# Attention with negated scores, the differential heads' norm moved among the units, and their rows combined before the division

## The reference, cut to what matters

```python
def diff_mixer(q, k, v, lam, lam_init, g_subln):
    ...
        logits = jnp.einsum('bqhcd,bshcd->bchqs', qb, k, preferred_element_type=jnp.float32) * scale
        logits = jnp.where(admissible[None, None, None], logits, -jnp.inf)
        p = jax.nn.softmax(logits, axis=-1)
        attn = p[:, 0] - lam * p[:, 1]
        return jnp.einsum('bhqs,bshe->bqhe', attn.astype(v.dtype), v)
    ...
    return rms_norm(out, g_subln) * (1.0 - lam_init)
...
mixed = jnp.concatenate([out_a, out_b], axis=-1)
x = x + jnp.einsum('bsc,cd->bsd', mixed, w_out[layer])
```

## Time and profile before

| | |
|---|---|
| median of 3 runs | 3076.5 us (3076.12 to 3080.77) |
| the profiled execution: its own time | 3079.2 us |
| its span | 3077.1 us |
| PE busy | 2821.8 us, 92% |
| DVE busy | 1800.8 us, 59% |
| ACT busy | 1132.6 us, 37% |
| granted PE clock, mean | 0.95 |

### The profile page before, as it was taken

How to read it: one execution, slowest core, us unless ns; L and a number is a source line. 1 busy time by engine, 2 the same in 40 slices (tenths; PEclk the granted TensorE clock), 3 DMA queues, 4 the chain that set the end, 5 groups by cost and what they waited for, 6 DMA issues and landing times.

```text
span 3077.1 us, 41761 instructions
## 1 busy us (share of the span) xinstructions
PE 2821.8 (92%) x16794; PEld 2132.6 (69%) x16794; DVE 1800.8 (59%) x3354; ACT 1132.6 (37%) x2024; POOL 151.4 (5%) x139
## 2 busy tenths in 40 slices
PE   7998977889999999999979976999999997899998
PEld 4887755775667667667637754788887764678887
DVE  4257866565677777777565787433334688443333
ACT  3323223222255556556513336322222325432222
POOL 0000000000012222212100000000000000000000
PEclk9998887889999999999999988999999997999999
DMA  6210002323368889899882200324222210222412
GB/s 222 83 57 19 1 1 72 115 58 142 120 262 337 345 349 357 344 359 347 311 328 99 83 7 1 117 69 130 70 86 105 83 62 1 83 69 76 137 52 72
DMA packets 180783, 433.08 MB, mean 141 GB/s; under 512 B 20131, under 2 KB 109542, under 8 KB 161254
## 3 DMA queue, kind: packets, MB, share of 16 engines
q1 hardware_dynamic: 161862, 396.72, 35.8%
q0 software_dynamic: 18720, 33.60, 2.9%
HBM read 426.56 MB, written 38.29 MB: 151 GB/s over the span
## 4 chain that ended last, share of the span: by engine, by line
PE 67%; DVE 10%; DMA 5%; ACT 3%; issue 2%; POOL 0%; SPq 0%; POOLq 0%; DVEq 0%; ACTq 0%
PE ps L298 15%; PE ps L299 15%; PE ps L300 15%; PE ps L2498 6%; DMA ring<-in_ew 2%; PE ps L2014 2%; PE ps L1506 2%; PE ps L2524 1%; DMA hg<-h_rows,idx 1%; DVE Pb L3405 1%; PE ps L2737 1%; PE ps L3137 1%; PE ps L2218 1%; DVE bi L3238 1%; DMA yr<-y_rows 1%
## 5 line engine op out<-in xcount | busy, mean ns | idle before, releaser
L2937 DVE TENSOR_TENSOR wf<-ring,wf 128x1024 fp32r<-128x1024 f32 (+1 forms) x152 | 181.6, 1197 | 336.8 <-ACT wf L2933 336.7
L2933 ACT ACTIVATE wf<-ring 128x1024 fp32r<-128x1024 f32 (+1 forms) x152 | 156.5, 1032 | 353.4 <-PE ps L300 353.4
L298 PE MATMUL ps<-hxh,wf 128*128 128x512 f32 x704 | 276.0, 392 | 2.8 <-DVE hxl L3082 2.8
L299 PE MATMUL ps<-hxl,wf 128*128 128x512 f32 x704 | 275.4, 391 | 0.0
L300 PE MATMUL ps<-hxh,wf 128*128 128x512 f32 x704 | 275.3, 391 | 0.0
L2436 DVE TENSOR_TENSOR spA<-ring,spA 128x1024 fp32r<-128x1024 f32 x156 | 184.5, 1222 | 102.7 <-ACT spA L2431 102.5
L2498 PE MATMUL ps<-ring,hdT 128*128 128x512 f32 x520 | 234.8, 594 | 0.8 <-issue 0.8
L2431 ACT ACTIVATE spA<-ring 128x1024 fp32r<-128x1024 f32 x156 | 157.7, 1053 | 50.1 <-DMA ring<-in_ew 42.9
L2436 DVE TENSOR_TENSOR spB<-ring,spB 128x1024 fp32r<-128x1024 f32 x104 | 124.3, 1222 | 68.4 <-ACT spB L2431 68.0
L2498 PEld LDWEIGHTS ps<-ring,hdT 128*128 128x128 f32 x520 | 93.8, 190 | 94.3 <-issue 91.4
L298 PEld LDWEIGHTS ps<-hxh,wf 128*128 128x128 f32 x704 | 133.2, 189 | 31.5 <-DVE hxl L3082 3.6
(11 more groups left out here) (615 smaller groups left out, 6222.5 us busy)
## 6 DMA issues: line engine op xcount, KB each, us to landing
ring<-in_ew SPq DMA_DIRECT2D x65, 2048.0 KB
ring<-in_ew SPq DMA_DIRECT2D x65, 1024.0 KB
ring<-in_w_in SPq DMA_DIRECT2D x17, 2048.0 KB, 7.8
ring<-in_w_gate SPq DMA_DIRECT2D x20, 1024.0 KB, 5.5
ring<-in_w_up SPq DMA_DIRECT2D x20, 1024.0 KB, 8.0
ring<-in_w_down SPq DMA_DIRECT2D x16, 1024.0 KB, 5.0
adaw<-in_ada_w SPq DMA_DIRECT2D x24, 512.0 KB, 6.2
ring<-in_w_out SPq DMA_DIRECT2D x6, 2048.0 KB, 7.8
```

The lines of the kernel that those rows point to most:

```text
L298: pe.matmul(o, lhs[0], rhs[0], start=start, stop=False)
L299: pe.matmul(o, lhs[0], rhs[1], start=False, stop=False)
L2933: act.activation(item_part(n)[0], item_raw(n), ACT.Copy).then_inc(*w_hi.inc(n))
L2937: v.tensor_tensor(item_part(n)[1], item_raw(n), f(item_part(n)[0]), ALU.subtract).then_inc(*w_lo.inc(n))
```

## The change

- `top` scales the scores by -0.125 and takes the minimum, so that no negation follows; the exponential gets scale -1.
- A differential unit is combined without division: `p0 + p1 * (sum0 * -lam / sum1)`; its row sum 0 stays in `esum`. The norm takes the factor: mean squares are multiplied twice by 1/`esum`, and the final scale once.
- Squares of the differential output stand in DVE's steps 21 to 24, the root in ACT's step 25, the scale in steps 27 to 31, the transposes in PE's steps 32 and 33, two of the four copies with gain in ACT's step 33.
- The first two weight splits of `W_out` stand in ACT's steps 17 and 18 and DVE's steps 25 and 26, in other buffers of `wf`.
- Behind the last unit ACT copies k = 0, 1, then the last two tiles with gain, then k = 2, 3, a split and k = 4 to 7. The output projection's first products wait for each tile alone.

```diff
+            nsq = sb("nsq", [128, 4, 128], c=s1)
+            esum = sb("esum", [128, 2, 16], c=s1)
...
-        s = wr[:, m % 2] if kind == "in" else wf[:, m % 4]
+        s = wr[:, m % 2] if kind == "in" else wf[:, (m + 2) % 4]
...
-        for i in range(4):
-            pe.wait_ge(*n_mul.val((l, i)))
-            for h in range(4):
-                m = pe.transpose(ps[i][:, h * 128:(h + 1) * 128], ob[:, i, h * 128:(h + 1) * 128], ident)
-            m.then_inc(*n_T.inc((l, i)))
+            for i in {32: (0, 1), 33: (2, 3)}.get(s, ()):
+                pe.wait_ge(*u_max.val((l, 31)))
+                pe.wait_ge(*n_mul.val((l, i)))
+                for h in range(4):
+                    m = pe.transpose(ps[i][:, h * 128:(h + 1) * 128], ob[:, i, h * 128:(h + 1) * 128], ident)
+                m.then_inc(*n_T.inc((l, i)))
 
     def attn_act(act, l):
+        n0 = first_of[l, "out"]
+
+        def rows_T(i0):
+            for i in (i0, i0 + 1):
+                act.wait_ge(*n_T.val((l, i)))
+                act.activation(ym_(l)[:, 4:8, i * 128:(i + 1) * 128], v4(ps[i][:, :]), ACT.Copy, scale=gsc[:, l:l + 1]).then_inc(*n_y.inc((l, i)))
...
-                    m = act.activation(p_, p_, ACT.Exp, bias=stt_[:, s % 4, 2 + c:3 + c], accum_out=stt_[:, s % 4, 4 + c:5 + c])
+                    m = act.activation(p_, p_, ACT.Exp, scale=-1.0, bias=stt_[:, s % 4, c:c + 1],
+                                       accum_out=esum[:, 0, s:s + 1] if UNITS[s][2] and c == 0 else stt_[:, s % 4, 4 + c:5 + c])
...
-        n0 = first_of[l, "out"]
-        for n in range(n0, n0 + 2):
-            split_hi(act, n)
+            if s in (17, 18):
+
+                act.wait_ge(*u_qk.val((l, 15)))
+                split_hi(act, n0 + s - 17)
+            if s == 25:
+                act.wait_ge(*n_sum.val(l))
+                act.activation(nrm[:, 1, :], nrm[:, 0, :], ACT.Sqrt, bias=EPS6, scale=1.0 / 128).then_inc(*n_sd.inc(l))
+            if s == 33:
+                rows_T(0)
         act.wait_ge(*u_out.val((l, 31)))
-        for k in range(4):
+        for k in range(8):
+            if k == 4:
+                act.wait_ge(*n_y.val((l, 3)))
+                split_hi(act, n0 + 2)
             act.activation(hx[0][:, k, :], ym_(l)[:, k, :], ACT.Copy).then_inc(*y_hi.inc((l, k)))
...
+            if k == 1:
+                rows_T(2)
...
             for c in range(2):
                 v.tensor_tensor_reduce(out=Pb[:, u % 4, c, 0:ns], in0=ps[2 * (u % 2) + c][:, 0:ns],
-                                       in1=zb[:, 512 - ns:512] if diff or i == 0 else bi[:, i - 1, 0:ns], scale=0.125, scalar=-3e38,
-                                       op0=ALU.add, op1=ALU.max, accum_out=s_[:, c:c + 1]).then_inc(*V.inc())
-            v.wait_ge(*V.val())
-            v.tensor_scalar(s_[:, 2:4], s_[:, 0:2], -1.0, None, ALU.mult).then_inc(*u_max.inc((l, u)))
+                                       in1=zb[:, 512 - ns:512] if diff or i == 0 else bi[:, i - 1, 0:ns], scale=-0.125, scalar=3e38,
+                                       op0=ALU.add, op1=ALU.min, accum_out=s_[:, c:c + 1]).then_inc(*(u_max.inc((l, u)) if c else V.inc()))
...
-            v.reciprocal(s_[:, 6:8], s_[:, 4:6]).then_inc(*V.inc())
-            v.wait_ge(*V.val())
             if diff:
-                v.tensor_tensor(s_[:, 7:8], s_[:, 7:8], lms[:, l, 7:8], ALU.mult).then_inc(*V.inc())
-                v.tensor_scalar(p0, p0, s_[:, 6:7], None, ALU.mult).then_inc(*V.inc())
+
+                v.reciprocal(s_[:, 7:8], s_[:, 5:6]).then_inc(*V.inc())
                 v.wait_ge(*V.val())
-                v.scalar_tensor_tensor(out=p0, in0=p1, scalar=s_[:, 7:8], in1=p0, op0=ALU.mult, op1=ALU.add).then_inc(*u_nrm.inc((l, u)))
+                v.scalar_tensor_tensor(out=s_[:, 6:7], in0=esum[:, 0, u:u + 1], scalar=s_[:, 7:8], in1=lms[:, l, 7:8], op0=ALU.mult,
+                                       op1=ALU.mult).then_inc(*V.inc())
+                v.wait_ge(*V.val())
+                v.scalar_tensor_tensor(out=p0, in0=p1, scalar=s_[:, 6:7], in1=p0, op0=ALU.mult, op1=ALU.add).then_inc(*u_nrm.inc((l, u)))
...
+        def squares(i):
+
+            v.wait_ge(*u_out.val((l, 4 * i + 3)))
+            v.wait_ge(*V.val())
+            for h in range(4):
+                o_, n = ob[:, i, 128 * h:128 * h + 128], 4 * i + h
+                m = v.tensor_tensor_reduce(out=nsq[:, h, :], in0=o_, in1=o_, scale=1.0, scalar=0.0, op0=ALU.mult, op1=ALU.add,
+                                           accum_out=nrm[:, 0, n:n + 1])
+            m.then_inc(*V.inc())
+            if i == 3:
+
+                v.reciprocal(esum[:, 1, :], esum[:, 0, :]).then_inc(*V.inc())
+                for k in range(2):
+                    v.wait_ge(*V.val())
+                    v.tensor_tensor(nrm[:, 0, :], nrm[:, 0, :], esum[:, 1, :], ALU.mult).then_inc(*(n_sum.inc(l) if k else V.inc()))
...
+            if 21 <= s < 25:
+                squares(s - 21)
+            if 25 <= s < 27:
+                split_lo(v, n0 + s - 25)
+            if s == 27:
+                v.wait_ge(*n_sd.val(l))
+                v.reciprocal(nrm[:, 0, :], nrm[:, 1, :]).then_inc(*V.inc())
+                v.wait_ge(*V.val())
+                v.tensor_tensor(nrm[:, 0, :], nrm[:, 0, :], esum[:, 1, :], ALU.mult).then_inc(*V.inc())
+            if 28 <= s < 32:
+                if s == 28:
+                    v.wait_ge(*V.val())
+                i = s - 28
+                v.tensor_tensor(v4(ob[:, i, :]), v4(ob[:, i, :]), bc(nrm[:, 0, 4 * i:4 * i + 4], 128), ALU.mult).then_inc(*n_mul.inc((l, i)))
+        for k in range(8):
             v.wait_ge(*y_hi.val((l, k)))
             v.tensor_tensor(hx[1][:, k, :], ym_(l)[:, k, :], f(hx[0][:, k, :]), ALU.subtract).then_inc(*y_lo.inc((l, k)))
...
+            if k == 3:
+                split_lo(v, n0 + 2)
...
-                if hf == 0 and kp == 0:
-                    pe.wait_ge(*n_y.val((l, 3)))
                 for i in range(4):
+                    if hf == 0 and kp == 0:
+                        pe.wait_ge(*n_y.val((l, i)))
                     m = part(hf, kp, i)
```

More of the change, by code:

```diff
@@ L3416, in normal @@
             v.wait_ge(*u_exp.val((l, u)))
-            v.reciprocal(s_[:, 6:8], s_[:, 4:6]).then_inc(*V.inc())
-            v.wait_ge(*V.val())
             if diff:
-                v.tensor_tensor(s_[:, 7:8], s_[:, 7:8], lms[:, l, 7:8], ALU.mult).then_inc(*V.inc())
-                v.tensor_scalar(p0, p0, s_[:, 6:7], None, ALU.mult).then_inc(*V.inc())
+                v.reciprocal(s_[:, 7:8], s_[:, 5:6]).then_inc(*V.inc())
                 v.wait_ge(*V.val())
-                v.scalar_tensor_tensor(out=p0, in0=p1, scalar=s_[:, 7:8], in1=p0, op0=ALU.mult, op1=ALU.add).then_inc(*u_nrm.inc((l, u)))
-            else:
+                v.scalar_tensor_tensor(out=s_[:, 6:7], in0=esum[:, 0, u:u + 1], scalar=s_[:, 7:8], in1=lms[:, l, 7:8], op0=ALU.mult,
+                                       op1=ALU.mult).then_inc(*V.inc())
+                v.wait_ge(*V.val())
+                v.scalar_tensor_tensor(out=p0, in0=p1, scalar=s_[:, 6:7], in1=p0, op0=ALU.mult, op1=ALU.add).then_inc(*u_nrm.inc((l, u)))
+            else:
+                v.reciprocal(s_[:, 6:8], s_[:, 4:6]).then_inc(*V.inc())
+                v.wait_ge(*V.val())
                 v.tensor_scalar(p0, p0, s_[:, 6:7], None, ALU.mult).then_inc(*V.inc())
                 v.tensor_scalar(p1, p1, s_[:, 7:8], None, ALU.mult).then_inc(*u_nrm.inc((l, u)))
+        n0 = first_of[l, "out"]
+        def squares(i):
[11 more added lines that the diff above has]
+                    v.tensor_tensor(nrm[:, 0, :], nrm[:, 0, :], esum[:, 1, :], ALU.mult).then_inc(*(n_sum.inc(l) if k else V.inc()))
         rest = IDX[sum(IDX_DVE):]
```

## The result

The changed kernel takes 3061.17 us (median of 4 runs, 3054.74 to 3066.3) beside 3078.64 us (4 runs, 3076.12 to 3083.41): a ratio of 0.9943, interval 0.993 to 0.9957, 17.5 us less. Forecast were 25.6 us less, 3051 with a range from 3044 to 3060. The direction was right and the median lies just outside the range. Of the 10.2 us between 3051 and 3061.17, 2.1 come from the base: the forecast started from 3076.5, and the kernel before has 3078.64 with its fourth run.

A forecast was written before the change was run, and what follows sets the result against it. DVE bounds the differential units, a ring of waits the selective ones, serial work the tail. Per layer -6.4 + 3.0 - 10.7 + 1.3 = -12.8, two layers -25.6: from 3076.5 to 3051 us, range 3044 to 3060.

The forecast's parts named there:

- rival of 0.03: Output projection begins and stays at low clock: all gain gone from 27% of it, 3144 us if all; chance 0.03.
- sign of failure: Forecast fails if the clock is low in wide differential units, or stretch two grows by more than 6 us per layer.
- The price list: Times of the old tail's work groups, used to price work moved among selective units, such as 0.9 us per squares group.
- Differential units: First attention stretch: negation and pass over p0 save 8.0 us of DVE, PE takes back 1.6; net -6.4 per layer.
- Selective units and drain: Second stretch: added work 4.8 less 1.6 for the negation, taken as +3.0 per layer; 16 transposes in the drain add 2.0.
- Tail: Behind the last unit: 14.6 us removed, 1.9 stays for copies and subtraction; with 2.0 for transposes, net -10.7 per layer.
- norm: Norm behind the output projection: a serial square-root table load between square and root, +1.3 us per layer.
- The rival with twice the time per load: Three table loads per layer on the path hold ACT 1.3 us more each: +7.8, 3059 us; chance 0.04.

The follow-up runs named there:

- table ahead: Changed kernel plus one square root of a constant behind the output projection's last weight split, loading the root's table early: 3055.98 us, ratio 0.9935.
- weight splits behind: Changed kernel with the first two splits of W_out moved back behind the last unit, on ACT and DVE: 3063.89 us, ratio 0.9946.

## Why the prediction was wrong

**The step that failed is the clock.** It said that the projection starts in a high clock because "only 2 us of idle time precede it", and held a low clock there for a rival of 0.03 that stays low throughout. It starts high, falls 1 us later and comes back 3 to 4 us after that, which costs 1.6 us per layer: 3.2. Its other reason, that today's projection starts high behind 10.4 us of idle time, does not carry: behind the same 10.4 us the kernel with the negated scores alone lost 1.6 to 1.7 us in both layers. In the selective units it took the granted 1.00 of stretch two for given; the changed kernel falls to 1.2 GHz there in 7 of 8 profiled layers of the same code: behind the table loads in 4, in the narrow units in 3 (one layer has both), between the two in 1. One fall costs some 1.5 us, in the narrow units 2.5. In the profile of the result that is 2.5 us, and layer 1's selective stretch grew by 6.5 us, which the prediction had named as a sign of failure (more than 6). Why the clock falls in the narrow units, right behind an idle time of only 0.8 us, stays open. The price list by itself, without clock, would have been better than the forecast: per layer -6.2 + 4.0 - 12.5 + 1.3 = -13.4, or 27 us. The clock took 5.7 of them back (4.7 and 7.4 in two other profiles of the same selective code with the same idle time of 2.4 us).

The clock alone does not account for the miss. The medians differ by 17.5 us, the attention stages by 21.4; the other 4 us lie ahead of attention and have no shown cause (last paragraph of this section). By an estimate from these numbers, either of the two, taken away, would have put the median inside the range: 3061.2 - 5.7 = 3055.5, or 3057.

**Differential units** (-6.4 forecast, -6.1 and -6.4 measured): right, by errors that cancel. The negation was worth 0.19 us in each step, as read. But from first top to first top the stretch holds 16 tops and 15 `normal`s, not 17 and 16: unit 15's comes behind the border. That is 0.2 and 0.4 us less than the 8.0 counted. The 128x1 operation takes 0.22 us where its neighbour took 0.16, so 0.44 us and not 0.38 pass to the combining pass: 0.9 us less over 15 units. DVE's saving was 6.5, not 8.0. PE took back not 1.6 but 0.30 us, at the first 384-column scores, since its clock was high in the other wide units (in layer 0 from 1831.9 on). That was stated as the condition ("0 if the clock is high then"); why it stays high is only argued: PE does the same work in less time.

**Selective units and drain** (+5.0 forecast, +3.95 without a fall of the clock). Transposes 2.0: right. Loads 2.0 for 1.5, splits 0.7 for 0.9, the negation 1.35 (layer 1 of its own run) or 1.6 (taken back from the changed kernel) for 1.6. That leaves 0.6 to 0.9 for the squares and their small products: 3.95 - 2.0 - 2.0 - 0.7 + 1.35 or 1.6. They were priced at 2.4. No run left them out alone; the remainder is a difference of others.

**Tail** (-12.7 forecast, -12.5 measured) and **norm** (+1.3, +1.27): right. The run with the table ahead shows the second by itself.

**Table loads.** The rival with twice the time per load is out: root 1.30 us behind its load (1883.16 to 1884.46), 2.9 us for two loads and a root, and the first load starts as the copy ahead of it ends. But the advice of the page "ScalarE: Activation LUTs" of the Trainium skill (Table sets: the hidden batching unit), all exponentials before the roots, was weighed only by the load's length. The run that follows it is 18 us faster than the changed kernel by the medians, of which 12.2 lie in the attention stages.

**What is left over.** The attention stages save 21.4 us in one pair of profiles and 19.7 in the other, the medians 17.5 and 15.4. The difference, about 4 us, lies by the profiles in the stage ahead of attention, whose time varies from execution to execution. Whether part of it is a property of the changed program stays open: both profiles of the changed kernel were executions above its median.

## What to carry to other kernels

A saving on the engine that binds a stretch raises the busy share of the others. Where TensorE runs at 1.2 GHz for part of that stretch, it can become the one that is waited for, and two savings together can be worth more than their sum: here 6.2 us per layer for 2.5 and 2.7, and no gain in the kernel's time for each alone. Before moving work into gaps, look at what the gaps of TensorE become: an idle time of 2.4 us ahead of dense matmuls cost 1.6 us of clock beside its own length in 8 of 10 layers, one of 2.87 us among the units 1.5 us in 9 of 14. With some 1 us of the 2.4 filled, even with needless transposes, no such fall came in 8 layers. A root among exponentials is paid three times here: two loads in the middle and one at the next root.

## What the runs showed of the hardware

- The fall from 2.4 to 1.2 GHz is not tied to the moment at which work begins again. In the profile of the result: idle until 1916.15, full speed to 1917.14, then 0.43 us per product until 1920.50. Over the ten layers with a slow projection in the changed kernel and its variants, the granted clock fell from 0.5 us before the first product (weight splits behind, 4.96 us idle) to 1.5 us behind it (root's table ahead, 2.40 us idle).
- The tail of the kernel before, with 10.4 us of idle time, ran its transposes at 1.2 GHz (0.42 us each), and yet its projection was granted 2.4 GHz from its first product on; in the run with the negated scores alone the same tail was followed by 1.6 us of loss. The page "TensorE: Matmul & The Clock Gate" of the Trainium skill (Part 1: The HAM clock gate) says that the gate's window is free-running and does not start anew with a kernel. That the same tail ended both ways agrees with it; no run here sets it apart from other causes.
- A `scalar_tensor_tensor` of 128x1 took 0.22 us beside 0.16 for a `tensor_tensor` of the same size.
